# Two transformer blocks on one core: x's second half waited for later, pairs of weight units ended one after the other, pool mixing on four PSUM tiles

## The chip, the cores and the metric

The kernel runs on one NeuronCore of a Trainium2 chip. The metric is the device time of one execution in microseconds (us). Five engines work side by side: TensorE (PE, matrix products), VectorE (DVE), ScalarE (ACT), GpSimd (POOL) and SyncE (SP, which here only issues transfers). They meet through semaphores.

## The reference

The program computes two different blocks, each two layers deep, for 512 tokens of 1024 channels in float32. The first block also carries a context stream of 256 tokens, so that in its first layer each product runs over 768 tokens, and in its second layer over 512.

```python
for l in range(DEPTH):                       # first block
    ml = ada_mod(c, w_ada[l], b_ada[l], 6)   # modulation vectors
    hl = modulate(x, ml[..., 0, :], ml[..., 1, :])
    zl = hl @ w_in[l] + b_in[l]              # q, k, v, conv, pool input, gates
    ...
    outs.append(win_sum / cnt - uf[:, :, sl])                 # multiscale pool, 4 windows
    mixed = jnp.einsum('blgi,gio->blgo', pooled, pool_w)      # the mixing, 4 groups of 256 channels
    m = gates[..., 0, :] * attn_o + gates[..., 1, :] * conv_o + gates[..., 2, :] * pool_o
    x = layer_norm(ALPHA * x + ml[..., 2, :] * (m @ w_out + b_out))
    x = layer_norm(ALPHA * x + ml[..., 5, :] * ffn(modulate(x, ml[..., 3, :], ml[..., 4, :])))
for i in range(DEPTH):                       # second block
    u = rmsnorm(h, ln_mix[i]) @ w_in[i]
    h = h + jnp.concatenate([y_mla, y_gla], axis=-1) @ w_out[i]
    gate = jax.nn.sigmoid(rmsnorm(h, ple_norm[i]) @ w_ple_gate[i])
    h = h + gate * (p[i] @ w_ple_proj[i])
```

## The kernel before

**Products.** Activations stand with channels on the partitions, in 8 chunks of 128. Each float32 product is made of three passes: high half of the weights by high half of the activations (`WH`, `XH`), low by high (`WL`, `XH`), high by low (`WH`, `XL`). A weight *unit* holds 8 blocks of 128 x 128, so one unit gives one output chunk. Units go through a ring of 4 slots: SP loads them into one of two raw buffers, ACT writes the high half (`weight_hi`, L1176, semaphore `hi_done`), and POOL (L464) or, in two stages, DVE (`low_half`, L1856) writes the low half (`units_split`). PE counts `units_used`.

**PSUM.** There are four tiles of 1024 columns. `tile_free[t]` counts their releases by ACT or DVE. `STAGES` lists for each stage of the program how often it uses each tile, from which `taken` and `emptied` work out the counts to wait for. Most stages alternate between two tiles: unit n of a stage waits until unit n-2 has been read out.

**Pairs.** Where a stage begins before its activations are all there, the first two units are computed together, chunk by chunk: `first_pair` in the first block (L503; stages conv, pw, out, up0, down0, down1, down2, so 7 in each layer) and `paired` in the second block (L842; ina, w_out, pg). For each chunk k the order is pass 0 of both units, pass 1 of both, pass 2 of both. The third unit then needs the tile of the first (in ina it has another tile).

**Mixing (L798).** For each of the 4 pool groups PE makes two output chunks, on tiles 0 and 1; ACT (L1410) reads both out when both are done. The groups' inputs (`pooled`) come from DVE's `pool_windows`.

**Entry.** SP issues 16 pieces of the modulation weights (512 KB each), the small tables, two weight units and then x in two halves (L417). PE sums the modulation vectors (L674), ACT copies the sums (`ada_copy`, L1315), PE turns them (`ada_turned`, L684), DVE adds the bias (L1997), and then ACT and DVE make the high and low halves of the first stage's input (L1330, L2135, L2141), and the first pair runs (L503). PE's wait ahead of `ada_turned` is

```python
pe.wait_ge(loaded, 6 * 16)
```

and `loaded` counts the five small tables and x's second half. Behind the first pair PE makes two more modulation steps (`ada_ahead`, L674), whose last weights come into `tmp`, a buffer that is free once the low halves of all 8 chunks are written.

Of the kernel before, what the change touches and what calls it, by code (L numbers as in the profile page):

```python
# [24 lines left out]
P = 128  # L25
# [32 lines left out]
X_AT = ({j: (2 * j - 6, 2 * j - 5) for j in range(3, 7)}, {2: (0, 1), 3: (2, 3), 4: (4, 5), 5: (6, 7)})  # L58
UQ_ITEMS = (4, 5, 0, 1, 2, 3, "rope0", "rope1", "rope2", 6, 7, 8, 9, 10, 11, 12, 13)
# [22 lines left out]
for _l in range(LAYERS):  # L82
    if _l == 0:
        STAGES += [((_l, "ada"), 0, (0, 0, 0, 1))]
    STAGES += [((_l, "ada_rest"), 0, (0, 0, 1, 1)), ((_l, "conv"), 4, (8, 8, 0, 0)), ((_l, "gate0"), 2, (4, 4, 0, 0)),
               ((_l, "qkv"), 3, (6, 6, 3, 10)), ((_l, "attn"), 0, (16, 16, 32, 16))]
    if _l == 0:
        STAGES += [((_l, "attn_ctx"), 0, (8, 8, 16, 8))]
    STAGES += [((_l, "u"), 2, (4, 4, 0, 0)), ((_l, "mix"), 0, (4, 4, 0, 0)), ((_l, "gate2"), 2, (4, 4, 0, 0)), ((_l, "cln"), 0, (0, 0, 2, 2)),
               ((_l, "gate1"), 2, (4, 4, 0, 0)), ((_l, "pw"), 2, (0, 0, 4, 4)), ((_l, "out"), 2, (4, 4, 0, 0)),  # L90
               ((_l, "ln1"), 0, (1, 0, 2, 1))]
# [39 lines left out]
def two_blocks(nc, weights, ada_w, pool_w, vec1_d, vec2_d, gla_w_d, x_d, cond_d, ple_d, pos_d, consts_d, rope_d,  # L131
# [4 lines left out]
    with ctx:  # L136
# [132 lines left out]
        cond_loaded, loaded = sem("conditions_loaded"), sem("params_loaded")  # L269
# [116 lines left out]
        def _(sp):  # L386
# [71 lines left out]
        def _(pool):  # L458
# [7 lines left out]
            for r0, r1 in ((RING[0, "conv"], RING[0, "conv"] + 1), (RING[0, "qkv"] + 1, RING[1, "conv"] + 1), (RING[1, "qkv"] + 1, ROUNDS)):  # L466
                if r0:
                    pool.wait_ge(units_split, r0 * SLOTS)
# [6 lines left out]
        def _(pe):  # L475
            def linear(l, st, rounds, sp_, kt=CH, hi=XH, lo=XL, ready=None, ahead=None, behind=None, within=None, by_chunk=False, tb=0):
# [17 lines left out]
                def first_pair():  # L494
                    start(0, 0)
                    start(0, 1)
                    for k in range(kt):
                        for n, (w, act) in enumerate(((WH, hi), (WL, hi), (WH, lo))):
                            if n != 1:
                                pe.wait_ge(*at_least(l, ready[n // 2][0], ready[n // 2][1] + k + 1))  # L500
                            for s in range(2):
                                for a, b in sp_:
                                    last = nc.tensor.matmul(ps(tb + s, a, b), w[:, s * UNIT + k * P:s * UNIT + (k + 1) * P],  # L503
                                                            act[:, k * TOK + a:k * TOK + b],
                                                            start=(n == 0 and k == 0), stop=(n == 2 and k == kt - 1))
                                if n == 2 and k == kt - 1:
                                    last.then_inc(units_used, 1)
# [214 lines left out]
            def block1(l):  # L722
                sp_, W = spans(l), width(l)
                if l == 0:
# [6 lines left out]
                    pe.wait_ge(loaded, 6 * 16)  # L731
# [59 lines left out]
                for g in range(4):  # L791
                    pe.wait_ge(*at_least(l, "pooled", 2 * g + 2))
                    for o in range(2):
                        pe.wait_ge(tile_free[o], taken(l, "mix", o, g))
                        for k in range(2):
                            w0 = POOLW + ((2 * g + o) * 2 + k) * P
                            for a, b in sp_:
                                last = nc.tensor.matmul(ps(o, a, b), AR[:, w0:w0 + P],  # L798
# [38 lines left out]
            def block2(l):  # L837
# [6 lines left out]
                def paired(st, hi, lo, n, ks, ready, before=None):  # L844
# [4 lines left out]
                    for at_, k in enumerate(ks):  # L849
                        if before:  # L850
                            before(k)
                        for i, (w, act) in enumerate(((WH, hi), (WL, hi), (WH, lo))):
                            if i == 0:
                                pe.wait_ge(*at_least(l, ready[0], ready[2](k)))
                            if i == 2:
                                pe.wait_ge(*at_least(l, ready[1], ready[2](k)))
                            for s in range(2):
                                last = products(ps(s, 0, SEQ), w, act, slot_of(l, st, s) * UNIT + k * P, n, k, i == 0 and at_ == 0, i == 2 and at_ == CH - 1)
                                if i == 2 and at_ == CH - 1:
                                    last.then_inc(units_used, 1)  # L860
# [303 lines left out]
        def _(act):  # L1164
# [642 lines left out]
            for s in range(2):  # L1807
# [11 lines left out]
        def _(dve):  # L1819
# [294 lines left out]
            def block1(l):  # L2114
                W = width(l)
                if l == 0:
                    dve.wait_ge(on(0, "ada_image"), 1)
# [8 lines left out]
                if l == 0:  # L2126

                    dve.wait_ge(x_half, 16)
                    for i in range(CH // 2):
                        if i == CH // 4:  # L2130
                            dve.wait_ge(loaded, 6 * 16)
# [661 lines left out]
```

## Time and profile before

| | |
|---|---|
| median of 3 runs | 3341.41 us (3340.28 to 3343.42) |
| profiled execution | 3340.82 us |
| its span, first to last instruction | 3339.0 us |
| mean granted clock of TensorE | 0.981 of 2.4 GHz |
| busy: PE / DVE / ACT / POOL | 96% / 59% / 34% / 25% |

The profiled execution's time is its span and 1.8 us around it. Busy time is an average over stages. Idle time of PE is listed in the trace with the operation whose end released it; an operation behind which a chain hangs moves with everything ahead of it.

### The profile page before, as it was taken

How to read it: one execution, taken by the hardware profiler on the slowest of the kernel's cores; microseconds unless marked ns; L12 is line 12 of the kernel's file. 1: busy time of each engine (PE TensorE's matmuls, PEld its weight loads, DVE VectorE, ACT ScalarE, POOL GpSimd, SP SyncE). 2: the span in 40 equal slices, each digit the busy share in tenths (PEclk: the TensorE clock that was granted, in tenths of full speed). 3: DMA queues.
4: the chain of work that ended last, by engine and by line, in shares of the span. 5: the costliest groups of instructions: out<-in, count | busy, mean ns of one | idle time of the engine just before them, and what ended most of it. 6: DMA issues, size and time to landing. Idle time of an engine off the chain costs nothing.

```text
span 3339.0 us, 43512 instructions
## 1 busy us (share of the span) xinstructions
PE 3207.3 (96%) x16010; PEld 2520.0 (75%) x16010; DVE 1953.8 (59%) x2687; ACT 1138.2 (34%) x1615; POOL 848.3 (25%) x336
## 2 busy tenths in 40 slices
PE   6999999999989999998999999999999999999998
PEld 4778777788878888886777767688886776777765
DVE  4887886654566253457888885583466525344333
ACT  2122254233233121223234435442225334442433
POOL 1001201233323232230020134354443231332312
PEclk8999999999999999999999999999999899999999
DMA  7442101112111111124520023232322210221211
GB/s 269 161 168 76 51 1 32 44 57 101 57 46 61 64 63 63 63 69 167 209 78 26 32 75 114 73 99 91 96 92 85 70 63 21 93 82 51 70 38 63
DMA packets 75307, 270.50 MB, mean 81 GB/s; under 512 B 8592, under 2 KB 9616, under 8 KB 74512
## 3 DMA queue, kind: packets, MB, share of 16 engines
q1 hardware_dynamic: 71376, 256.04, 23.0%
q10 hardware_dynamic: 3776, 12.32, 1.0%
q8 instruction: 107, 1.75, 0.2%
q14 instruction: 48, 0.39, 0.0%
HBM read 263.87 MB, written 4.46 MB: 80 GB/s over the span
## 4 chain that ended last, share of the span: by engine, by line
PE 85%; DVE 8%; DVEq 2%; ACT 2%; issue 1%; DMA 1%; SPq 0%; ACTq 0%
PE ps L537 48%; PE ps L842 12%; PE ps L503 4%; PE ps L653 2%; PE ps L776 2%; PE ps L983 1%; DVE arena L2061 1%; PE ps L953 1%; PE ps L674 1%; PE ps L641 1%; PE ps L798 1%; DVE x L2069 1%; PE ps L1062 1%; PE ps L756 1%; PE ps L1082 1%
## 5 line engine op out<-in xcount | busy, mean ns | idle before, releaser
L464 POOL TENSOR_TENSOR w_lo<-w_raw,w_hi 128x1024 fp32r<-128x1024 f32 x332 | 848.1, 2558 | 2455.2 <-ACT w_hi L1176 2455.1
L1176 ACT ACTIVATE w_hi<-w_raw 128x1024 fp32r<-128x1024 f32 x380 | 399.1, 1054 | 556.0 <-PE ps L537 297.2
L537 PE MATMUL ps<-act_hi,w_hi 128*128 128x512 f32 (+1 forms) x2608 | 552.3, 361 | 7.6 <-ACT arena L1410 1.8
L537 PE MATMUL ps<-act_lo,w_hi 128*128 128x512 f32 (+1 forms) x2608 | 536.2, 355 | 0.0
L537 PE MATMUL ps<-act_hi,w_lo 128*128 128x512 f32 (+1 forms) x2608 | 535.3, 354 | 0.0
L537 PEld LDWEIGHTS ps<-act_hi,w_hi 128*128 128x128 f32 x2608 | 427.7, 188 | 126.8 <-issue 50.9
L537 PEld LDWEIGHTS ps<-act_hi,w_lo 128*128 128x128 f32 x2608 | 428.3, 188 | 72.5
L537 PEld LDWEIGHTS ps<-act_lo,w_hi 128*128 128x128 f32 x2608 | 428.3, 188 | 72.4 <-issue 0.5
L1909 DVE SCALAR_TENSOR_TENSOR x<-ps,mod,x 128x512 f32<-128x512 f32 x96 | 60.2, 659 | 295.5 <-PE ps L537 238.2
L2069 DVE SCALAR_TENSOR_TENSOR x<-arena,vec,x 128x512 f32<-128x512 f32 x336 | 230.5, 714 | 0.0
L2061 DVE SCALAR_TENSOR_TENSOR arena<-arena,vec 128x783 f32<-128x783 f32 (+1 forms) x240 | 228.0, 950 | 0.2 <-issue 0.2
L2292 DVE SCALAR_TENSOR_TENSOR arena<-arena,vec 128x769 f32<-128x769 f32 (+1 forms) x88 | 160.4, 1823 | 16.0 <-issue 16.0
L1242 ACT ACTIVATE arena<-ps,vec 128x768 f32<-128x768 f32 (+3 forms) x64 | 50.8, 794 | 281.5 <-PE ps L537 195.1
L842 PE MATMUL ps<-act_hi,w_hi 128*128 128x512 f32 x432 | 127.5, 432 | 9.2 <-ACT act_hi L1522 6.2
L1830 DVE TENSOR_TENSOR ffn_lo<-arena,ffn_hi 128x768 f32 (+1 forms) x44 | 119.0, 2704 | 6.5
L842 PEld LDWEIGHTS ps<-act_hi,w_hi 128*128 128x128 f32 x432 | 86.3, 206 | 38.6 <-issue 19.8
L842 PE MATMUL ps<-act_hi,w_lo 128*128 128x512 f32 x432 | 112.8, 395 | 0.0
L842 PE MATMUL ps<-act_lo,w_hi 128*128 128x512 f32 x432 | 111.6, 392 | 0.0
L776 PE MATMUL ps<-arena 128*128 128x256 f32 (+1 forms) x288 | 102.4, 475 | 5.9 <-ACT tmp L1281 5.9
L2289 DVE TENSOR_SCALAR arena<-arena,vec 128x769 f32<-128x769 f32 (+1 forms) x44 | 29.1, 661 | 132.4 <-ACT arena L1494 132.4
L1494 ACT ACTIVATE arena<-ps 128x512 f32<-128x512 f32 x66 | 32.4, 526 | 213.8 <-PE ps L537 211.1
L653 PE MATMUL ps<-arena 128*128 128x256 f32 x416 | 103.1, 381 | 1.6 <-ACT arena L1398 1.5
(336 smaller groups left out, 4494.5 us busy)
## 6 DMA issues: line engine op xcount, KB each, us to landing
w_raw<-in_weights SPq DMA_DIRECT2D x380, 512.0 KB, 3.5
arena<-in_ada_w SPq DMA_DIRECT2D x75, 512.0 KB, 4.6
tmp<-in_ada_w SPq DMA_DIRECT2D x21, 512.0 KB, 4.4
x<-in_x SPq DMA_DIRECT2D x2, 1536.0 KB, 19.9
x<-in_x ACTq DMA_DIRECT2D x1, 3072.0 KB, 10.8
arena<-in_pool_w ACTq DMA_DIRECT2D x2, 1024.0 KB, 4.9
x_mid<-x ACTq DMA_DIRECT2D x1, 2048.0 KB, 7.4
x<-x_mid ACTq DMA_DIRECT2D x1, 2048.0 KB, 8.5
```

The costliest lines, as they stand in the source:

```text
L464: nc.gpsimd.tensor_tensor(WL[:, w], raw, WH[:, w].bitcast(f32), ALU.subtract).then_inc(units_split, 1)
L503: last = nc.tensor.matmul(ps(tb + s, a, b), w[:, s * UNIT + k * P:s * UNIT + (k + 1) * P], act[:, k * TOK + a:k * TOK + b], start=(n == 0 ...
L537: last = nc.tensor.matmul(ps(t, a, b), w[:, s * UNIT + k * P:s * UNIT + (k + 1) * P], act[:, k * TOK + a:k * TOK + b], start=(n == 0 and k ...
L653: last = nc.tensor.matmul(ps(3, (m % 2) * 512, (m % 2) * 512 + 2 * P), values(m, k), AR[:, a:a + 2 * P], start=(k == 0), stop=(k == nk - 1))
L776: last = nc.tensor.matmul(ps(it % 2, a, b), AR[:, q:q + P], AR[:, k + a:k + b], start=True, stop=True)
L842: return nc.tensor.matmul(out, w0[:, k0:k0 + P], act[:, k * n:k * n + SEQ], start=start, stop=stop)
L1176: nc.scalar.activation(WH[:, s * UNIT:(s + 1) * UNIT], RAW[:, (s % 2) * UNIT:(s % 2 + 1) * UNIT], ACT.Copy).then_inc(hi_done, 1)
L1830: return V.tensor_tensor(lo, src, hi.bitcast(f32), ALU.subtract)
L1909: last = V.scalar_tensor_tensor(x, ps(t, a, b), at(MOD, mod(l, gate, j, m), 1), x, ALU.mult, ALU.add)
L2061: t = V.scalar_tensor_tensor(acc, src, w, acc, ALU.mult, ALU.add)
L2069: t = V.scalar_tensor_tensor(acc, src, w, acc, ALU.mult, ALU.add)
L2292: t = V.scalar_tensor_tensor(cv, src, w, cv, ALU.mult, ALU.add)
```

## The change

It has four parts.

1. x's second half is counted on the semaphore of the conditions (`cond_loaded`) and no longer on `loaded`. PE waits for the five tables alone ahead of `ada_turned`; ACT and DVE wait for the second half at chunk 4. SP waits for the conditions' activation before it issues x.
2. The low halves of the first four units go from POOL to DVE: two ahead of the modulation vectors, two behind the last low half of x. ACT makes the high half of unit 1 behind `ada_copy`.
3. In the last chunk of each pair the three passes of unit 0 come first, then the three of unit 1.
4. The mixing takes tiles 0 and 1 for even groups, 2 and 3 for odd ones.

```diff
+ORDER_OF_PAIR = (((0, 0), (0, 1), (1, 0), (1, 1), (2, 0), (2, 1)), ((0, 0), (1, 0), (2, 0), (0, 1), (1, 1), (2, 1)))
...
-    STAGES += [((_l, "u"), 2, (4, 4, 0, 0)), ((_l, "mix"), 0, (4, 4, 0, 0)), ...
+    STAGES += [((_l, "u"), 2, (4, 4, 0, 0)), ((_l, "mix"), 0, (2, 2, 2, 2)), ...
...
-            for k, landed in enumerate((x_half, loaded)):
+            sp.wait_ge(on(0, "cond"), 1)
+            for k, landed in enumerate((x_half, cond_loaded)):
...
-            for r0, r1 in ((RING[0, "conv"], RING[0, "conv"] + 1), (RING[0, "qkv"] + 1, RING[1, "conv"] + 1), (RING[1, "qkv"] + 1, ROUNDS)):
+            for r0, r1 in ((RING[0, "qkv"] + 1, RING[1, "conv"] + 1), (RING[1, "qkv"] + 1, ROUNDS)):
...
-                        for n, (w, act) in enumerate(((WH, hi), (WL, hi), (WH, lo))):
-                            if n != 1:
+                        for n, s in ORDER_OF_PAIR[k == kt - 1]:
+                            w, act = ((WH, hi), (WL, hi), (WH, lo))[n]
+                            if n != 1 and s == 0:
                                 pe.wait_ge(*at_least(l, ready[n // 2][0], ready[n // 2][1] + k + 1))
...
-                    pe.wait_ge(loaded, 6 * 16)
+                    pe.wait_ge(loaded, 5 * 16)
...
-                        pe.wait_ge(tile_free[o], taken(l, "mix", o, g))
+                        t = 2 * (g % 2) + o
+                        pe.wait_ge(tile_free[t], taken(l, "mix", t, g // 2))
...
-                        for i, (w, act) in enumerate(((WH, hi), (WL, hi), (WH, lo))):
+                        for i, s in ORDER_OF_PAIR[at_ == CH - 1]:
...
-                            act.wait_ge(loaded, 6 * 16)
+                            act.wait_ge(cond_loaded, 2 * 16)
...
-                    nc.scalar.activation(AR[:, B0 + c * TOK:B0 + c * TOK + W], ps(c % 2, 0, W), ACT.Copy,
-                                         scale=v1(l, "pool_scale", c)).then_inc(tile_free[c % 2], 1)
+                    nc.scalar.activation(AR[:, B0 + c * TOK:B0 + c * TOK + W], ps(c % 4, 0, W), ACT.Copy,
+                                         scale=v1(l, "pool_scale", c)).then_inc(tile_free[c % 4], 1)
...
-            for s in range(2):
-                weight_hi(0, s)
+            weight_hi(0, 0)
             ada_copy(0, False)
+            weight_hi(0, 1)
...
                 if l == 0:
+                    low_half(0)
+                    low_half(1)
                     dve.wait_ge(on(0, "ada_image"), 1)
...
+                    low_half(2)
+                    low_half(3)
```

The order on the engines, at three places. On DVE, at the start of the program, this stood ahead of the modulation vectors (`mod`):

```order
L2652 MEMSET ones_in_first_column 128x1
L1997 TENSOR_TENSOR mod<-ps,vec 128x32
L2003 TENSOR_SCALAR mod<-mod 128x16
L2121 TENSOR_SCALAR qk_bias<-vec 128x8
L2122 TENSOR_SCALAR qk_bias<-vec 128x2
```

and this stands there now:

```order
L2656 MEMSET ones_in_first_column 128x1
L1856 TENSOR_TENSOR w_lo<-w_raw,w_hi 128x1024 x2
L1997 TENSOR_TENSOR mod<-ps,vec 128x32
L2003 TENSOR_SCALAR mod<-mod 128x16
L2123 TENSOR_SCALAR qk_bias<-vec 128x8
L2124 TENSOR_SCALAR qk_bias<-vec 128x2
```

The low halves of units 0 and 1 have come in ahead of the vectors; those of units 2 and 3 stand in the same way between the last `act_lo` and the memset of the convolution's buffer.

On PE, the last chunk of the first pair of stage conv (two column spans, 512 and 256, for each unit and pass) was

```order
L503 MATMUL ps<-act_hi,w_hi 128x512
L503 MATMUL ps<-act_hi,w_hi 128x256
L503 MATMUL ps<-act_hi,w_hi 128x512
L503 MATMUL ps<-act_hi,w_hi 128x256
L503 MATMUL ps<-act_hi,w_lo 128x512
L503 MATMUL ps<-act_hi,w_lo 128x256
L503 MATMUL ps<-act_hi,w_lo 128x512
L503 MATMUL ps<-act_hi,w_lo 128x256
L503 MATMUL ps<-act_lo,w_hi 128x512
L503 MATMUL ps<-act_lo,w_hi 128x256
L503 MATMUL ps<-act_lo,w_hi 128x512
L503 MATMUL ps<-act_lo,w_hi 128x256
```

and is now

```order
L504 MATMUL ps<-act_hi,w_hi 128x512
L504 MATMUL ps<-act_hi,w_hi 128x256
L504 MATMUL ps<-act_hi,w_lo 128x512
L504 MATMUL ps<-act_hi,w_lo 128x256
L504 MATMUL ps<-act_lo,w_hi 128x512
L504 MATMUL ps<-act_lo,w_hi 128x256
L504 MATMUL ps<-act_hi,w_hi 128x512
L504 MATMUL ps<-act_hi,w_hi 128x256
L504 MATMUL ps<-act_hi,w_lo 128x512
L504 MATMUL ps<-act_hi,w_lo 128x256
L504 MATMUL ps<-act_lo,w_hi 128x512
L504 MATMUL ps<-act_lo,w_hi 128x256
```

The same twelve products; unit 0 ends behind the sixth of them and no longer behind the tenth.

On PE, the second and third group of the mixing in layer 0, with the semaphores that they wait for, began

```order
L798 MATMUL ps<-arena 128x512 [waits tile_free0,block0_pooled]
L798 MATMUL ps<-arena 128x256
L798 MATMUL ps<-arena 128x512
L798 MATMUL ps<-arena 128x256
L798 MATMUL ps<-arena 128x512 [waits tile_free1]
```

in both, and the second begins now

```order
L800 MATMUL ps<-arena 128x512 [waits tile_free2,block0_pooled]
L800 MATMUL ps<-arena 128x256
L800 MATMUL ps<-arena 128x512
L800 MATMUL ps<-arena 128x256
L800 MATMUL ps<-arena 128x512 [waits tile_free3]
```

while the third goes back to tiles 0 and 1. Only the tiles waited for have moved.

## Rows read from the trace of the kernel before

**Rows 1.** The page's chain that ended last, by engine

```profile
PE 85%; DVE 8%; DVEq 2%; ACT 2%; issue 1%; DMA 1%; SPq 0%; ACTq 0%
```

**Rows 2.** Waits of PE, whole span: total us, times, longest

```profile
PE ps L720 <- DVE arena L2177: 7.1, 4, 3.9
PE ps L537 <- DVE x L1909: 7.0, 8, 1.1
...
PE ps L798 <- ACT arena L1410: 5.9, 6, 1.1
...
PE ps L842 <- DVE arena L2630: 2.4, 3, 1.0
...
PE ps L537 <- ACT arena L1410: 1.8, 2, 1.0
PE ps L537 <- DVE arena L2230: 1.7, 2, 0.9
...
PE ps L842 <- DVE x L2613: 1.3, 2, 0.6
PE ps L537 <- ACT arena L1494: 1.3, 2, 0.7
...
PE ps L537 <- ACT arena L1345: 0.6, 1, 0.6
```

**Rows 3.** Timeline, 28 to 42 us: start, length, engine; idle before and releaser

```profile
28.90 1.06 ACT L1176 ACTIVATE w_hi<-w_raw 128x1024 fp32r<-128x1024 f32 x1 [0.21 <-DMA w_raw<-in_weights]
...
29.99 0.60 ACT L1315 ACTIVATE arena<-ps 128x512 f32<-128x512 f32 x1
...
37.02 1.88 PE L684 MATMUL ps<-ident,arena 128*128 128x8 f32 x8 [7.11 <-DMA x<-in_x]
...
41.08 1.62 PE L503 MATMUL ps<-act_hi,w_hi 128*128 128x512 f32 x4 [2.18 <-ACT act_hi L1330]
```

**Rows 4.** SP's two transfers of x: starts, and issue to landing

```profile
L417 SPq DMA_DIRECT2D x<-in_x x2: 433/1458/2483, 14.6 to 15.1; - x2
...
DMA to landing us min/median/max: 17.9/19.9/21.9
```

**Rows 5.** Timeline, 44 to 66 us, the first pair and what follows

```profile
44.09 1.65 DVE L2135 TENSOR_SCALAR tmp<-x,mod 128x512 f32<-128x512 f32 x4
...
50.45 5.65 POOL L464 TENSOR_TENSOR w_lo<-w_raw,w_hi 128x1024 fp32r<-128x1024 f32 x2 [16.86 <-ACT w_hi L1176]
...
51.39 5.64 DVE L2135 TENSOR_SCALAR tmp<-x,mod 128x512 f32<-128x512 f32 x4
...
58.12 0.96 PE L503 MATMUL ps<-act_lo,w_hi 128*128 128x512 f32 x4 [0.82 <-DVE act_lo L2141]
...
61.13 1.06 PE L674 MATMUL ps<-arena,gla_w 128*32 128x512 f32 x8
63.01 0.62 PE L674 MATMUL ps<-arena,gla_w 128*32 128x512 f32 x2 [0.81 <-DMA tmp<-in_ada_w]
...
64.01 3.09 PE L537 MATMUL ps<-act_hi,w_hi 128*128 128x512 f32 x16
...
65.97 1.22 DVE L1856 TENSOR_TENSOR w_lo<-w_raw,w_hi 128x1024 fp32r<-128x1024 f32 x1
```

**Rows 6.** The page's DMA issues: count, KB each, us to landing

```profile
tmp<-in_ada_w SPq DMA_DIRECT2D x21, 512.0 KB, 4.4
```

**Rows 7.** Timeline, last chunk of up0's pair in layer 0

```profile
959.23 0.87 PE L503 MATMUL ps<-act_hi,w_lo 128*128 128x512 f32 x4
...
959.94 0.86 PE L503 MATMUL ps<-act_lo,w_hi 128*128 128x512 f32 x4
```

**Rows 8.** Timeline, the mixing: layer 0, then layer 1

```profile
620.19 5.40 PE L798 MATMUL ps<-arena 128*128 128x512 f32 x16 [1.08 <-ACT arena L1410]
...
1949.64 0.24 DVE L2110 TENSOR_TENSOR arena<-arena 128x8 f32<-128x8 f32 x2
...
1952.15 3.67 PE L798 MATMUL ps<-arena 128*128 128x512 f32 x8 [0.87 <-ACT arena L1410]
```

More of the change, by code:

```diff
@@ L88 @@
         STAGES += [((_l, "attn_ctx"), 0, (8, 8, 16, 8))]
-    STAGES += [((_l, "u"), 2, (4, 4, 0, 0)), ((_l, "mix"), 0, (4, 4, 0, 0)), ((_l, "gate2"), 2, (4, 4, 0, 0)), ((_l, "cln"), 0, (0, 0, 2, 2)),
+    STAGES += [((_l, "u"), 2, (4, 4, 0, 0)), ((_l, "mix"), 0, (2, 2, 2, 2)), ((_l, "gate2"), 2, (4, 4, 0, 0)), ((_l, "cln"), 0, (0, 0, 2, 2)),
                ((_l, "gate1"), 2, (4, 4, 0, 0)), ((_l, "pw"), 2, (0, 0, 4, 4)), ((_l, "out"), 2, (4, 4, 0, 0)),
@@ L266, in in2 @@
             return "inb", m, m % 2, m // 2 + (m > 6)
[L269 removed]
+        cond_loaded, loaded = sem("conditions_and_then_rest_of_x_loaded"), sem("params_loaded")
         x_half = sem("first_half_of_x_loaded")
@@ L464, in low_half @@
                 nc.gpsimd.tensor_tensor(WL[:, w], raw, WH[:, w].bitcast(f32), ALU.subtract).then_inc(units_split, 1)
-            for r0, r1 in ((RING[0, "conv"], RING[0, "conv"] + 1), (RING[0, "qkv"] + 1, RING[1, "conv"] + 1), (RING[1, "qkv"] + 1, ROUNDS)):
-                if r0:
-                    pool.wait_ge(units_split, r0 * SLOTS)
+            for r0, r1 in ((RING[0, "qkv"] + 1, RING[1, "conv"] + 1), (RING[1, "qkv"] + 1, ROUNDS)):
+                pool.wait_ge(units_split, r0 * SLOTS)
                 with loop(pool, r1 - r0) as r:
@@ L497, in first_pair @@
                     for k in range(kt):
-                        for n, (w, act) in enumerate(((WH, hi), (WL, hi), (WH, lo))):
-                            if n != 1:
+                        for n, s in ORDER_OF_PAIR[k == kt - 1]:
+                            w, act = ((WH, hi), (WL, hi), (WH, lo))[n]
+                            if n != 1 and s == 0:
                                 pe.wait_ge(*at_least(l, ready[n // 2][0], ready[n // 2][1] + k + 1))
-                            for s in range(2):
[L502 to L507, printed above, removed]
+                            for a, b in sp_:
+                                last = nc.tensor.matmul(ps(tb + s, a, b), w[:, s * UNIT + k * P:s * UNIT + (k + 1) * P],
+                                                        act[:, k * TOK + a:k * TOK + b],
+                                                        start=(n == 0 and k == 0), stop=(n == 2 and k == kt - 1))
+                            if n == 2 and k == kt - 1:
+                                last.then_inc(units_used, 1)
                 if ready:
@@ L797, in block1 @@
                             for a, b in sp_:
-                                last = nc.tensor.matmul(ps(o, a, b), AR[:, w0:w0 + P],
+                                last = nc.tensor.matmul(ps(t, a, b), AR[:, w0:w0 + P],
                                                         AR[:, B0 + (2 * g + k) * TOK + a:B0 + (2 * g + k) * TOK + b],
@@ L851, in paired @@
                             before(k)
-                        for i, (w, act) in enumerate(((WH, hi), (WL, hi), (WH, lo))):
[L853 to L860, printed above, removed]
+                        for i, s in ORDER_OF_PAIR[at_ == CH - 1]:
+                            w, act = ((WH, hi), (WL, hi), (WH, lo))[i]
+                            if i != 1 and s == 0:
+                                pe.wait_ge(*at_least(l, ready[i // 2], ready[2](k)))
+                            last = products(ps(s, 0, SEQ), w, act, slot_of(l, st, s) * UNIT + k * P, n, k, i == 0 and at_ == 0, i == 2 and at_ == CH - 1)
+                            if i == 2 and at_ == CH - 1:
+                                last.then_inc(units_used, 1)
                 def single(st, i, t, k_use, hi=XH, lo=XL, n=TOK, within=None):
@@ L1806, in _ @@
                                  ACT.Silu).then_inc(on(0, "cond"), 1)
-            for s in range(2):
-                weight_hi(0, s)
+            weight_hi(0, 0)
             ada_copy(0, False)
+            weight_hi(0, 1)
             act.dma_start(AR[:, COS:COS + 2 * SEQ], rope_d).then_inc(on(0, "rope_table"), 16)
@@ L2130, in block1 @@
                         if i == CH // 4:
-                            dve.wait_ge(loaded, 6 * 16)
+                            dve.wait_ge(cond_loaded, 2 * 16)
                         dve.drain()
```

## Prediction

> **What bounds the kernel now.** I read the chain that ended last first: 85% of the span hangs on PE, 8% on DVE [rows 1]. So an edit is worth what it takes out of PE's idle time, provided that nothing behind PE is late by itself. The second view is the list of PE's waits [rows 2]. Three groups in it belong to this change. Behind the pairs PE waits for the tile of unit 0: 7.0 us in 8 places for the residual, 1.7 in 2 for the merge, 1.3 in 2 for up0's copy, 0.6 in 1 for conv in layer 1, and in the second block 1.3 in 2 and two of the three waits on L2630. In the mixing it waits 5.9 us in 6 places for ACT's read-out, and 1.8 in 2 more at the first unit of gate2 behind it, which uses tile 0 too. The third view is the timeline of the entry: PE stands 7.11 us ahead of `ada_turned`, released by a transfer of x, though ACT's copy of the sums was over at 29.99 + 0.60 = 30.59 [rows 3].
>
> Not all waits are open to the change. L720's 7.1 us [rows 2] is time in which PE waits for DVE's norms; they begin only when PE hands them work, so I take that stretch to move as a whole.
>
> **Entry, up to the first pair.** What holds `ada_turned` falls away: of x's two halves, issued at 14.6 and 15.1, one landed 17.9 us and the other 21.9 us after its issue [rows 4]. In order that is 32.5 and 37.0, and 37.02 is when PE went on. The turning can start at 30.6 and ends 1.88 later, at 32.5. DVE now stands with two low halves ahead of the modulation vectors. The second needs ACT's high half of unit 1, now behind the copy: 30.59 + 1.06 = 31.65, and DVE's 1.22 [rows 3, 5] make 32.87, some 0.3 us later than PE's 32.5 and the hand-over. Queued behind it on DVE are the vectors, and on these wait ACT and PE. The gap from the end of the turning to the first pair was 41.08 - 38.90 = 2.18; so the pair starts at about 32.6 + 2.2 = 34.8 to 34.9, against 41.08: **6.2 us**. x's first half (32.5) is there before ACT asks for it; the second (37.0) is for chunk 4, which PE, at 2.1 us a chunk or more (three times the 0.71 of [rows 7]), does not reach before 43. SP's new wait on the conditions costs nothing: PE's sums, which ACT copies at 29.99, need the same activation, and the transfers issued ahead of x kept the queue busy until x landed.
>
> **Entry, the pair itself.** One chunk's low half held PE until 58.12, and the fourth part of the input on DVE had taken 5.64 where the part before took 1.65, beside two POOL operations of 5.65 together [rows 5]. POOL has nothing to do there now, so DVE gets 4.0 back. Chunk 6's low half would be ready at 58.12 - 4.0 - 6.2 = 47.9 and the last at about 48.9, well ahead of PE, which comes to the last chunk 2.1 us ahead of the pair's end, near 52. That gives the 0.82 us and the idle crumbs around it, about 1.0. The page SBUF — State Buffer of the Trainium skill (section Who interferes with whom) says that a DVE operation with two-port access and a GpSimd operation exclude each other for a whole instruction; the 5.64 agrees. The pair ends at 61.13 - 6.2 - 1.0 = 53.9.
>
> Behind the lows DVE makes the low halves of units 2 and 3, 1.22 each: 50.1 and 51.4. PE's third unit starts later than that, so cover is 3.8 us. But SP's next weight load waits for the first of them, and behind it in SP's queue stand the two modulation pieces that PE needs right behind the pair. The last went into `tmp` and held PE 0.81 us already [rows 5]. It would now be issued at about 50.2 + 0.6 + 0.6 = 51.5 and take 4.4 (the median of its kind [rows 6]): 55.9. PE gets there at 53.9 + 1.1 = 55.0, so a wait of 0.9 stays. PE's third unit then starts at about 56.9 in place of 64.01: **the entry gives 7.1 us**. If the piece lands at once, 7.9; if three transfers in a row take a microsecond longer, 6.1.
>
> **Pairs.** In layer 0, four products of the last chunk take 959.94 - 959.23 = 0.71 us [rows 7], so unit 0's last two and the same of unit 1 take 0.355 each. Before, unit 0 ended one such step ahead of the pair's end, now three: its tile comes free 0.71 earlier. The waits there are 0.65 to 1.1 [rows 2], so nearly all of it counts: 0.7 in pw, out, up0 and the three downs, 6 x 0.7 = 4.2. Conv in layer 0 has the modulation steps behind its pair and gives nothing. With 512 columns it is two thirds, 0.47: 7 pairs in layer 1, 4 of the second block's 6 (ina has another tile), 11 x 0.47 = 5.1, below each wait there. Sum **9.3**, of the 13 or so us waited. The low half of the last chunk is wanted one step and a half earlier, but where PE runs closest behind DVE, in up0, it went straight through [rows 7]. If the chunk's low half were late, that pair would give back up to 0.7.
>
> **Mixing.** The wait for tiles 0 and 1 goes where the group before used the other two: 3 x 1.08 + 1.0 = 4.2 us in layer 0, since a group's 5.40 us covers ACT's read-out of the group before [rows 2, 8]. In layer 1 it is 5.9 - 3.2 = 2.7 and 0.8. What is late next there is `pooled`: DVE ends the last chunk at 1949.88 [rows 8]; the fourth group began at 1952.15 and would like to begin 3 x 0.87 = 2.6 earlier, at 1949.5. So 0.4 comes back as a wait on DVE: 3.1. Sum **7.3**; DVE's taps behind gate2 begin with gate2's first read-out and move along.
>
> **Sum.** 7.1 + 9.3 + 7.3 = 23.7. The profiled execution (3340.82) goes to 3317.1; it stood 0.6 below the median, so I say **3317.7**. Its own range is 3314 to 3321: entry 6.1 to 7.9, pairs 8 to 9.3, mixing 6.5 to 7.7, and 1.5 us of spread between runs.
>
> **Rivals.**
> - *x's first half lands no earlier than the second* (10%). The four microseconds between the landings are read off two transfers [rows 4]. The page DMA: Bandwidth & Descriptors of the Trainium skill (section Queues, rings and completion order) says that completion is not in order of issue. As a mechanism here: the halves share the queue with the last weights, both are complete at 37.0, and ACT starts then. The pair starts at 37.0 + 2.2 = 39.2, the entry gives 1.9 + 1.0 = 2.9, and the time is 3321.9. For it: only the sum of the waits speaks, no engine waited for the first half. Against it: the two latencies, 17.9 and 21.9.
> - *The pairs and the mixing give half* (10%). Where DVE or ACT has a chain of its own behind the pair, an earlier tile only makes PE wait elsewhere. For it: L720's 7.1 us and the mixing's `pooled`. Against it: PE's waits end with the tile's read-out, and the read-outs start when PE's unit ends. Half of 16.6 is 8.3: 3326.0.
> - *Slower* (3%). In the stages where PE waits for DVE, each meeting of DVE with a POOL operation stretches a DVE operation by some 2 us (5.64 against 1.65 for two meetings [rows 5]). Moved phases could make more of them. It takes 12 new ones on the path to cancel 23.7, and 15 to be slower by over 0.2%, to 3348. POOL's work is released by ACT and this by PE, so they move together; that is why I give it little.
> - *The rest of the forecast* (77%) is the sum above.
>
> **Range and chances.** 0.2% is 6.7 us, about what a measurement of this kernel tells from none. 3313 to 3326 takes in the first two rivals' centres and all bounds. Faster 0.94, within 0.2% 0.03, slower 0.03.
>
> **What would show it.** `ada_turned` at 30.6 to 31 with no wait on x; the first pair at 34.8, DVE's four input parts all at 1.65 and no wait on `act_lo`; PE's third unit near 57. Waits behind the pairs of 0.2 to 0.4 in place of 0.7 to 1.1, in 17 places. No wait on L1410 in the mixing, one of 0.4 on DVE ahead of the last group in layer 1. The forecast is wrong if the act_hi of chunk 0 waits for x beyond 33, if PE waits for `units_split` at its third unit, or if the waits of rows 2 on L2177, L2021 or L1203 grow by what the others lose.

## The result and the profile after

| | before | after |
|---|---|---|
| median | 3342.41 us (3340.28 to 3344.83, 4 runs) | 3318.60 us (3317.08 to 3319.36, 4 runs) |
| profiled execution | 3340.82 us | 3319.36 us |
| its span | 3339.0 us | 3317.6 us |

The ratio is 0.993, 95% interval 0.9919 to 0.9942: faster by 0.7%. The medians lie 23.8 us apart (forecast 23.7; forecast time 3317.7, measured 3318.60), the two profiled executions 21.5 and their spans 21.4.

First the waits of PE in the changed kernel (total us, times, longest; L numbers are lines of the changed kernel, a few higher than in [rows 2]), against [rows 2].

```profile
PE ps L721 <- DVE arena L2181: 7.3, 4, 4.1
...
PE ps L675 <- DMA tmp<-in_ada_w: 3.9, 2, 2.2
...
PE ps L538 <- DVE x L1909: 2.3, 8, 0.4
...
PE ps L844 <- DVE arena L2634: 1.5, 3, 1.0
...
PE ps L800 <- DVE arena L2110: 0.7, 1, 0.7
...
PE ps L538 <- DVE arena L2234: 0.6, 2, 0.3
...
PE ps L844 <- DVE act_lo L2363: 0.4, 1, 0.4
...
PE ps L538 <- ACT arena L1345: 0.4, 1, 0.4
...
PE ps L844 <- DVE x L2617: 0.4, 2, 0.2
```

The eight waits for the residual fell from 7.0 to 2.3, the merge's two from 1.7 to 0.6, up0's copy (1.3) is gone, and so are both waits for the mixing's read-out (5.9 and 1.8). The norms' wait stayed, as said: 7.3 against 7.1. New are 0.7 in the mixing for the pool inputs and 0.4 in the first pair of the second block for a low half.

The timeline of the entry, 26 to 44 us (start, length, engine; idle before and releaser), against [rows 3]:

```profile
28.62 0.58 ACT L1315 ACTIVATE arena<-ps 128x512 f32<-128x512 f32 x1
...
29.34 1.03 PE L685 MATMUL ps<-ident,arena 128*128 128x8 f32 x8 [1.10 <-ACT arena L1315]
...
32.60 9.82 ACT L1330 ACTIVATE act_hi<-x,mod 128x512 fp32r<-128x512 f32 x16 [2.46 <-DMA x<-in_x]
...
34.05 1.62 PE L504 MATMUL ps<-act_hi,w_hi 128*128 128x512 f32 x4 [3.68 <-ACT act_hi L1330]
```

PE turns the vectors at 29.34 and waits for ACT's copy alone; before it went on at 37.02. ACT now has to wait for x's first half, which lands at 32.5 as in the kernel before. By the transfers' own group the two halves took as long as in [rows 4], within 0.4 us:

```profile
L419 SPq DMA_DIRECT2D x<-in_x x2: 432/1464/2495, 14.7 to 15.1; - x2
...
DMA to landing us min/median/max: 17.8/20.1/22.3
```

The timeline of the first pair's second half and what follows, 44 to 60 us, against [rows 5]:

```profile
43.68 1.65 DVE L2137 TENSOR_SCALAR tmp<-x,mod 128x512 f32<-128x512 f32 x4
...
47.16 2.35 DVE L1856 TENSOR_TENSOR w_lo<-w_raw,w_hi 128x1024 fp32r<-128x1024 f32 x2
...
49.73 0.33 SPq L391 DMA_DIRECT2D tmp<-in_ada_w  x1
...
52.67 1.06 PE L675 MATMUL ps<-arena,gla_w 128*32 128x512 f32 x8
...
55.94 0.62 PE L675 MATMUL ps<-arena,gla_w 128*32 128x512 f32 x2 [2.20 <-DMA tmp<-in_ada_w]
...
56.93 3.08 PE L538 MATMUL ps<-act_hi,w_hi 128*128 128x512 f32 x16
```

DVE's last part takes 1.65 and no longer 5.64, the low halves of units 2 and 3 follow at 47.16, and PE's third unit starts at 56.93 against 64.01.

The mixing, layer 0 and layer 1, in PE's timeline, against [rows 8]:

```profile
610.52 14.78 PE L800 MATMUL ps<-arena 128*128 128x512 f32 x45
...
1924.47 10.46 PE L800 MATMUL ps<-arena 128*128 128x512 f32 x24
1935.58 3.70 PE L800 MATMUL ps<-arena 128*128 128x512 f32 x8 [0.66 <-DVE arena L2110]
```

No gap is left in layer 0, and in layer 1 one, ahead of the last group, for DVE. Layer 0's first mixing product and the first product of gate2 behind it, in the kernel before:

```profile
613.78 5.33 PE L798 MATMUL ps<-arena 128*128 128x512 f32 x16
...
639.54 3.08 PE L537 MATMUL ps<-act_hi,w_hi 128*128 128x512 f32 x16 [0.99 <-ACT arena L1410]
```

The changed one starts gate2 here:

```profile
630.97 3.13 PE L538 MATMUL ps<-act_hi,w_hi 128*128 128x512 f32 x16
```

From start to start that is 25.76 us before and 20.45 (630.97 - 610.52) now, 5.31 less, though the waits taken out are 3 x 1.08 + 0.99 = 4.23.

Last, the span cut at the same two points of the program (PE's third unit of layer 1's first stage, and the first product of the second block). Behind the bounds stand the length, the busy time of PE, of its weight loads, DVE, ACT and POOL, and then the granted clock. The kernel before,

```profile
0.00:1534.06 1534.06, 1464.16 (x8165) 1202.82 (x8165) 919.43 (x1234) 448.11 (x600) 327.31 (x128) 0.99 0.24 81
1534.06:2538.88 1004.82, 969.90 (x4368) 750.60 (x4369) 694.70 (x877) 368.97 (x499) 309.00 (x120) 0.99 0.29 97
```

and the changed one:

```profile
0.00:1519.78 1519.78, 1463.92 (x8165) 1204.66 (x8165) 919.81 (x1238) 448.57 (x600) 324.65 (x124) 0.99 0.24 82
1519.78:2518.86 999.08, 969.32 (x4368) 751.14 (x4369) 692.01 (x877) 369.02 (x499) 309.39 (x120) 0.99 0.29 98
```

PE (the number behind the length) was busy for the same time in both, to 0.6 us. The first part is 14.28 us shorter and PE's idle time in it 14.0, the second part 5.74 and 5.2. What is left of the 21.4 lies behind, 1.4: the second block's products take 2.4 less, and the exit 1.0 more, because its last two products took 2.08 in place of 1.12. So in sum the two executions differ by idle time; the granted clock moved a few microseconds between stretches, in both directions, as is shown below.

### The profile page after: what moved, and what is told of

Its sections match the earlier page's. It is cut to its first block, busy times and chain, and to the rows that moved or that the text cites. A ratio compares the mean times of both kernels' runs of the same rounds, so it can differ in the third digit from the quotient of the medians.

```text
span 3317.6 us, 43566 instructions
## 1 busy us (share of the span) xinstructions
PE 3206.8 (97%) x16010; PEld 2521.2 (76%) x16010; DVE 1949.2 (59%) x2691; ACT 1138.4 (34%) x1615; POOL 846.1 (26%) x332
## 4 chain that ended last, share of the span: by engine, by line
PE 85%; DVE 9%; DVEq 2%; ACT 2%; issue 1%; DMA 1%; SPq 0%; ACTq 0%
PE ps L538 48%; PE ps L844 12%; PE ps L504 4%; PE ps L654 2%; PE ps L777 2%; PE ps L983 1%; DVE arena L2061 1%; PE ps L675 1%; PE ps L642 1%; PE ps L953 1%; DVE x L2069 1%; PE ps L1062 1%; PE ps L757 1%; PE ps L1082 1%; PE ps L587 1%
## 5 line engine op out<-in xcount | busy, mean ns | idle before, releaser
L1909 DVE SCALAR_TENSOR_TENSOR x<-ps,mod,x 128x512 f32<-128x512 f32 x96 | 60.3, 659 | 291.3 <-PE ps L538 238.2
```

Source lines behind the costliest of these rows:

```text
L1909: last = V.scalar_tensor_tensor(x, ps(t, a, b), at(MOD, mod(l, gate, j, m), 1), x, ALU.mult, ALU.add)
```

## The experiments

Medians are compared with the kernel before, timed beside each group of versions: 3341.86 us (28 runs) for the first four, 3340.48 (9 runs) for the next four, 3341.33 (9) for the three after them, 3340.89 (7) for the last.

**The entry alone.** The order of the pairs and the mixing stay as before.

```diff
-ORDER_OF_PAIR = (((0, 0), (0, 1), (1, 0), (1, 1), (2, 0), (2, 1)), ((0, 0), (1, 0), (2, 0), (0, 1), (1, 1), (2, 1)))
+ORDER_OF_PAIR = (((0, 0), (0, 1), (1, 0), (1, 1), (2, 0), (2, 1)), ((0, 0), (0, 1), (1, 0), (1, 1), (2, 0), (2, 1)))
```

> The entry alone (semaphores of x, low halves of the first four units on DVE, the high half of unit 1 behind the copy of the sums); pairs and mixing as before. Theory (the three parts add up, each worth the idle time it takes from PE): 7.1 us less than the kernel before, PE's third unit of stage conv starting at 56.9 us. Rival (the entry's gain is eaten in the attention of layer 0, where the changed kernel was seen to lose 2.5 us of its lead): 4.6 us less, with the lead shrinking between 380 and 415 us. A second rival, that the parts interact: less than 4 us or more than 10.

3336.77 us (11 runs), ratio 0.9981, interval 0.9972 to 0.9991: 5.1 us between medians, 6.3 by the ratio. The interval, 3.0 to 9.4 us, holds both the theory's 7.1 and the rival's 4.6; what decides between them is under "The sum by parts" below. Its timeline around the pair:

```profile
30.68 1.03 PE L685 MATMUL ps<-ident,arena 128*128 128x8 f32 x8 [0.82 <-ACT arena L1314]
...
34.72 1.62 PE L504 MATMUL ps<-act_hi,w_hi 128*128 128x512 f32 x4 [3.00 <-ACT act_hi L1329]
...
51.08 0.33 SPq L391 DMA_DIRECT2D tmp<-in_ada_w  x1
...
54.03 1.06 PE L675 MATMUL ps<-arena,gla_w 128*32 128x512 f32 x8
...
57.29 0.62 PE L675 MATMUL ps<-arena,gla_w 128*32 128x512 f32 x2 [2.19 <-DMA tmp<-in_ada_w]
```

Turning, pair and pair's end stand where the prediction put them (30.6, 34.8, 53.9). The piece in `tmp` doesn't: issued at 51.08 (forecast 51.5), PE could use it 6.2 us later, not 4.4. The third unit starts at 58.28.

**The order of the pairs alone.**

```diff
+ORDER_OF_PAIR = (((0, 0), (0, 1), (1, 0), (1, 1), (2, 0), (2, 1)), ((0, 0), (1, 0), (2, 0), (0, 1), (1, 1), (2, 1)))
...
-                        for n, (w, act) in enumerate(((WH, hi), (WL, hi), (WH, lo))):
-                            if n != 1:
+                        for n, s in ORDER_OF_PAIR[k == kt - 1]:
+                            w, act = ((WH, hi), (WL, hi), (WH, lo))[n]
+                            if n != 1 and s == 0:
```

> The order inside the last chunk of each pair alone; entry and mixing as before. Theory: 9.3 us less than the kernel before, PE's waits on L1909 down from 7.0 to about 2.3 us and those behind the other pairs to 0.2 to 0.4 each. Rival (DVE or ACT has a chain of its own behind the pairs): half or less, about 4.6 us, with other waits of PE longer.

3335.30 us (11 runs), ratio 0.9978 (0.9969 to 0.9987): 7.4 us by the ratio, with 4.3 to 10.4 in the interval, so the forecast 9.3 and the rival's 4.6 both fit the time, and the waits have to decide. PE's waits behind the pairs are those of the full change (the eight on x fell to 2.3 here too):

```profile
PE ps L843 <- DVE arena L2629: 1.5, 3, 1.0
...
PE ps L538 <- DVE arena L2229: 0.6, 2, 0.3
...
PE ps L538 <- ACT arena L1344: 0.5, 1, 0.5
...
PE ps L843 <- DVE x L2612: 0.4, 2, 0.2
```

**The mixing alone.**

```diff
-    STAGES += [((_l, "u"), 2, (4, 4, 0, 0)), ((_l, "mix"), 0, (4, 4, 0, 0)), ...
+    STAGES += [((_l, "u"), 2, (4, 4, 0, 0)), ((_l, "mix"), 0, (2, 2, 2, 2)), ...
...
-                        pe.wait_ge(tile_free[o], taken(l, "mix", o, g))
+                        t = 2 * (g % 2) + o
+                        pe.wait_ge(tile_free[t], taken(l, "mix", t, g // 2))
```

> The four tiles in the mixing alone. Theory: 7.3 us less than the kernel before (4.2 in layer 0, 3.1 in layer 1), no wait of PE on ACT's read-out in the mixing, and one of 0.4 to 0.7 us on DVE's pooled input ahead of the last group of layer 1. Rival (what is won comes back at the next wait on DVE, the sums of the convolution in layer 1, where PE waits 1.0 us): 4.2 us less and that wait at about 4 us.

3331.63 us (6 runs), ratio 0.9969 (0.9956 to 0.9981): 10.4 us by the ratio, the forecast 7.3 inside its interval (6.3 to 14.7 us). The rival's wait for the convolution's sums stayed at 1.0. The mixing of layer 1:

```profile
1934.67 10.46 PE L799 MATMUL ps<-arena 128*128 128x512 f32 x24
1946.01 3.70 PE L799 MATMUL ps<-arena 128*128 128x512 f32 x8 [0.88 <-DVE arena L2111]
```

The three ratios add up to 24.1 us, the full change gives 23.4 by its own: no sign that the parts lean on one another, within what three intervals of 3 to 4 us each way can tell.

**The entry's semaphores alone.** x's second half is waited for later, but the low halves of the first four units stay on POOL and ACT's order stays.

```diff
-            for k, landed in enumerate((x_half, loaded)):
+            sp.wait_ge(on(0, "cond"), 1)
+            for k, landed in enumerate((x_half, cond_loaded)):
...
-                    pe.wait_ge(loaded, 6 * 16)
+                    pe.wait_ge(loaded, 5 * 16)
```

> The entry's semaphores alone: x's second half no longer holds the turning of the sums; the low halves of the first four units stay on POOL and ACT's order stays. Theory (the 5.6 us operation on DVE beside POOL costs, apart from the wait on x): 6.3 us less than the kernel before, with PE waiting about 0.8 us for act_lo and DVE's fourth part of the input again at 5.6. Rival (the low halves on POOL cost nothing, the wait on x is all): the same as the whole entry, 7.1 us less, third unit at 56.9.

3335.54 us (11 runs), ratio 0.9981 (0.9972 to 0.999), the same as the whole entry; an interval of 3.3 to 9.4 us can't part the theory's 6.3 from the rival's 7.1. Its timeline:

```profile
29.15 4.65 POOL L466 TENSOR_TENSOR w_lo<-w_raw,w_hi 128x1024 fp32r<-128x1024 f32 x2 [28.70 <-ACT w_hi L1176]
...
32.36 1.47 DVE L2003 TENSOR_SCALAR mod<-mod 128x16 f32<-128x16 f32 x1
...
35.44 1.62 PE L505 MATMUL ps<-act_hi,w_hi 128*128 128x512 f32 x4 [3.47 <-ACT act_hi L1330]
...
45.75 5.62 DVE L2135 TENSOR_SCALAR tmp<-x,mod 128x512 f32<-128x512 f32 x4
...
53.49 0.33 SPq L391 DMA_DIRECT2D tmp<-in_ada_w  x1
...
57.02 0.62 PE L676 MATMUL ps<-arena,gla_w 128*32 128x512 f32 x2 [0.49 <-DMA tmp<-in_ada_w]
...
58.02 2.26 PE L539 MATMUL ps<-act_hi,w_hi 128*128 128x512 f32 x11
```

With POOL at work the pair starts 0.7 later and DVE's fourth part takes 5.62 again, so the piece for `tmp` is issued 2.4 later than with the low halves on DVE. But it lands after 3.4 us in place of 6.1, and PE waits 0.49 for it in place of 2.19. The third unit starts at 58.02, 0.3 ahead of the kernel with the whole entry. So neither the theory nor the rival had it: the 5.6 us operation costs in the pair, and taking it away gained nothing, because the transfer behind gave all of it back.

**The changed kernel with units 2 and 3 back on POOL.**

```diff
+            pool.wait_ge(units_split, 2)
+            for s in (2, 3):
+                low_half(0, s)
...
-                    low_half(2)
-                    low_half(3)
```

> The changed kernel with the low halves of units 2 and 3 on POOL again (units 0 and 1 stay on DVE). Theory, from the runs of the entry (the third unit began at 58.3 us with all four on DVE and at 58.0 with all four on POOL): what DVE wins in the pair comes back as a longer wait for the modulation piece in tmp, so the third unit starts within 0.6 us of the changed kernel's 56.9, DVE's fourth part of the input again taking 5.6 and the wait for tmp about 1 us shorter. Rival (the forecast's): DVE's 4 us count, PE waits 0.8 us for act_lo and the third unit comes 1 us or more later, near 58.

3317.42 us (5 runs), ratio 0.993 (0.9917 to 0.9944), that of the change itself. Its third unit starts at 57.70, between the theory's bound (57.5) and the rival's 58; DVE's fourth part takes 5.66, PE waits 0.52 for `act_lo` and 0.55 for the piece. But in this profile the pair began only at 35.07, against 34.05, because PE's last modulation sums ran at the lower clock (2.77 us for ten products against 1.48). From the pair's start to the third unit it is 22.6 us here, 22.9 in the changed kernel: the same trade once more.

**The changed kernel with the two modulation pieces ahead of the weight load** in SP's queue, at the one step where both stand.

```diff
-                        unit_load(r + (RING[l, st] + (s + 3) // SLOTS), (s + 3) % SLOTS)
+                        ada_first = l == 0 and st == "conv" and s == 1
+                        if not ada_first:
+                            unit_load(r + (RING[l, st] + (s + 3) // SLOTS), (s + 3) % SLOTS)
...
+                        if ada_first:
+                            unit_load(r + (RING[l, st] + (s + 3) // SLOTS), (s + 3) % SLOTS)
```

> The changed kernel with two transfers exchanged in SP's queue: the two modulation pieces that PE needs behind the first pair go ahead of the weight unit that waits for the low half of unit 2. Theory (the 2.2 us wait for tmp is the queue behind that unit's wait and transfer): the piece is issued at about 47.3 us and lands near 51.3, the wait is gone, the third unit starts at 54.8, and the whole is 2.1 us less than the changed kernel. Rival (the unit loaded later is missed instead): no gain, with PE waiting for a unit of stage conv or ACT's high halves late by more than 3 us.

3315.80 us (5 runs), ratio 0.9922 (0.9908 to 0.9935). The piece is issued at 47.56, lands 3.5 us later and nobody waits for it:

```profile
47.56 0.33 SPq L391 DMA_DIRECT2D tmp<-in_ada_w  x1
...
52.59 1.48 PE L679 MATMUL ps<-arena,gla_w 128*32 128x512 f32 x10
...
54.44 3.10 PE L542 MATMUL ps<-act_hi,w_hi 128*128 128x512 f32 x16
```

The third unit starts 2.5 us earlier than in the changed kernel (56.93), with the pair at the same place. So it was the transfer that held it. This profile does not carry the lead to the end: in the norms of layer 1 PE waited 2.7 us that most profiles don't have (10.0 in 5 places on the norms, where the changed kernel has 7.3 in 4), and it came to the second block at 2519.1, as the changed kernel did; a second profile of the same version, below, came there at 2513.3.

**The changed kernel with the last two chunks by unit** in the pairs where a wait was left (pw, out, the downs, w_out, pg).

```diff
-                    for k in range(kt):
-                        for n, s in ORDER_OF_PAIR[k == kt - 1]:
+                    by_unit = 2 if tb == 2 or st == "out" else 1
+                    steps = [(k, n, s) for k in range(kt - by_unit) for n, s in ORDER_OF_PAIR[0]]
+                    steps += [(k, n, s) for s in range(2) for k in range(kt - by_unit, kt) for n in range(3)]
+                    for k, n, s in steps:
...
+                    by_unit = 1 if st == "ina" else 2
```

> The changed kernel with the last two chunks of the pair by unit instead of the last one, in stages pw, out, the downs, w_out and pg. Theory (each remaining wait behind a pair is the rest of the read-out that three more products of 128 x 512 hide): PE's waits on L1909, on the merge, on w_out's and on pg's residual go from 3.8 us together to under 0.5, and the time is 3.5 us less than the changed kernel. Rival (the chunks' low halves come too late for unit 0 where DVE is close): new waits for act_lo or ffn_lo of as much.

3316.75 us (5 runs), ratio 0.9925 (0.9911 to 0.9938): the waits on L1909 and L2234 are gone, with them 2.9 us, those on the second block's residuals too (two of three on L2634, both on L2617), as the theory has it, 0.4 more came at `act_lo`, and the median moved by less than the runs' spread and not by 3.5. The second block's products (first and last start behind the colon), in the changed kernel and in this one:

```profile
L844 PE MATMUL ps<-act_hi,w_hi x432: 387/393/796, 2518.9 to 3233.1; 128*128 128x512 f32 x144
```

```profile
L846 PE MATMUL ps<-act_hi,w_hi x432: 387/389/796, 2511.1 to 3234.6; 128*128 128x512 f32 x144
```

It enters the second block 7.8 us ahead, more than the 2.9 of the waits and so partly for other reasons (two profiles of the version before it were 5.8 apart here), and leaves it 1.5 behind. The granted clock (the third number from the right) tells where most of it went, in the same two kernels:

```profile
3000.00:3100.00 100.00, 99.62 (x507) 79.19 (x508) 30.05 (x58) 26.05 (x39) 20.61 (x10) 0.86 0.15 48
```

```profile
3000.00:3100.00 100.00, 99.62 (x481) 79.07 (x480) 26.35 (x53) 25.62 (x39) 18.80 (x8) 0.80 0.12 43
```

PE is busy throughout in both, but ran longer at the lower of its two levels, and got through fewer instructions. Such windows of fixed time hold somewhat different work in each kernel. Cut by work, the products that the kernel before makes from 3000 to 3100 us took 106.0 us in this kernel at a clock of 0.84, and 100.1 in the changed one at 0.90, as in the kernel before (100.0 at 0.90).

**Both additions together.**

> Both: the two transfers exchanged and the last two chunks by unit. Theory: the gains add, 5.6 us less than the changed kernel, about 3313. Rival: less than 3 us, with the difference in a stage where PE's clock was granted low or in a new wait.

3315.05 us (5 runs), ratio 0.992 (0.9906 to 0.9933): not the 3313 of gains that add. The stretch just named took 106.0 us here too, at 0.84.

**Three kernels side by side**, since the versions above were not timed beside the change: the changed kernel, the one with both additions, and the one with the earlier pieces alone.

> The changed kernel once more, in one call with the version that has all four parts and two additions. Expected 3318 to 3319 us, some 23 us below the kernel before, with its third unit at 56.9 again.

> The changed kernel with the two modulation pieces ahead of the weight load in SP's queue and two chunks by unit where the pair's waits were left. If the piece in the temporary buffer was what held the third unit (2.2 us of waiting) and the tiles' read-outs the rest (2.3 + 0.6 + some 1 us), it is 5 to 6 us below the changed kernel of this call; the first reading gave 3.5 us between medians of two calls. If the third unit only moves a wait to a later place, as the rival has it, the difference is under 2 us. The kernel that has the first addition alone should stand 2.5 us below the changed kernel by its third unit, 54.44 against 56.93.

> The changed kernel with the two modulation pieces ahead of the weight load in SP's queue alone: 2.5 us below the changed kernel of this call if the 2.5 us at the third unit last to the end, 0 if the norms of DVE or the exit take them back.

The changed kernel took 3317.03 us (3316.09 to 3318.47), with both additions 3314.45 (3313.63 to 3316.93), with the earlier pieces alone 3314.02 (3312.58 to 3318.14); 5 runs each. The earlier pieces give 3.0 us between medians against the 2.5 expected, though the ranges overlap, and in these two profiles the third unit stood 1.3 apart (56.75 and 55.42), not 2.5. With both additions it is 2.6, neither the 5 to 6 of the theory nor the rival's under 2: the two chunks give nothing on top.

**Two chunks by unit in the first block alone**, with the earlier pieces.

```diff
-                    by_unit = 1 if st == "ina" else 2
+                    by_unit = 1
```

> The version with both additions, but with two chunks by unit in the first block's pairs alone; the second block's pairs keep the change's order. In the kernel with both, PE came to the second block 2.1 us ahead of the one without the two chunks (2511.2 against 2513.3) and left its last products 1.4 us behind it (3228.7 against 3227.3), while the granted clock from 3000 to 3100 us was 0.83 against 0.87. If the order inside the second block's pairs lowers that clock, it goes back to 0.86 or 0.87 here and the time falls to about 3312. If it is only where the phases of the second block come to stand, which the earlier arrival alone decides, the clock stays at 0.83 there and the time at 3314 to 3315.

3311.88 us (3309.39 to 3314.20, 4 runs), ratio 0.991 (0.9894 to 0.9927): the lowest median of all versions, 29.0 us below the kernel before timed beside it. The interval overlaps that of the earlier pieces alone (0.991 to 0.9937), so it isn't shown to be faster than they are. From 3000 to 3100 us the kernel with both additions (first fence) had 0.83, this one (second) 0.86:

```profile
3000.00:3100.00 100.00, 99.62 (x474) 78.38 (x473) 25.64 (x51) 25.69 (x38) 19.00 (x9) 0.83 0.13 47
```

```profile
3000.00:3100.00 100.00, 99.62 (x498) 78.81 (x499) 26.78 (x54) 27.69 (x41) 21.57 (x10) 0.86 0.14 48
```

This is what the theory of the order inside the second block's pairs expected, in clock and in the median. The profiled execution itself was the slowest of the four (3314.20, against 3314.45 for the profile with both additions), so clock and gain were not seen in one execution. By work the evidence is stronger: the products of that stretch took 104.5 to 106.0 us in the three profiles with two chunks in the second block, at 0.84 to 0.85, and 99.9 to 100.1 in all eleven others, this version's among them, at 0.90. The rival is not out. The three came to the second block at 2511.0 to 2511.2 us, the eleven between 2513.3 and 2538.9, this version at 2513.3; no kernel with the change's order arrived as early as the three.

## Why the prediction held, and where a size was off

**Turning and pair.** Right. x's first half was there at 32.5 and the second did not matter: the rival of halves that land together is out (the two halves landed apart in all 14 profiles, after 17.8 to 17.9 and 21.7 to 22.3 us). The full change turned 1.3 us earlier than said (29.34), with PE's last modulation sums run at the full clock in that execution (ten products in 1.48 us, in the kernel before 2.77); ACT then stood against x's first half, so only 0.75 of it reached the pair (34.05). In the entry alone the turning came at 30.68 and the pair at 34.72, as forecast.

**The pair itself.** I put its gain at 1.0. The pair, from its start up to the modulation step at 52.67, took 18.6 us against 20.05: 1.4. In the entry alone it took 19.3: 0.7. DVE's four parts are all 1.65 in both and neither waits for `act_lo`; the changed kernel's clock rose 0.4 us sooner in the second chunk, and its products then followed each other 2% faster.

**Behind the pair: the term that was mis-sized.** "Take 4.4 (the median of its kind)", and from it "a wait of 0.9 stays". The piece for `tmp` was issued at 49.73, 1.8 ahead of my 51.5, since DVE was done earlier. It took 6.2, not 4.4, and landed at 55.9, to the tenth what I had. PE came 1.3 earlier than I had it, and so it waited 2.2. Two errors of 1.8 cancelled in the landing, and with it in the third unit: 56.93 against 56.9. The entry alone shows the size without the luck: PE at the place forecast, 6.2 from the issue to PE's start, a wait of 2.19 and the third unit at 58.28, 1.4 late. 4.4 is the median of 21 transfers of its kind in one profile, and not even this piece's own time there, 3.7. By the landing itself the same piece took 5.6 to 6.2 in the four profiles where it is issued 0.6 us behind another piece and 1.2 behind a weight load, all of 512 KB, and 3.4 to 3.7 in the ten where everything ahead of it was issued 4.8 us or more before. A duration taken from a median has to be one of transfers with the same neighbours.

**Pairs.** Right in place, and in size by the waits: these are 0.2 to 0.4 in 15 places and gone in two (up0's copy). The one of conv in layer 1 fell from 0.64 to 0.44 alone, where I took off 0.47: unit 0 was done at 1518.65, but ACT was issuing a transfer (L1514) until 1518.90 and read out from 1518.95. New is that ina's pair waits 0.44 for a low half, at 2526.53 in its fourth chunk, which the new order doesn't touch: that product starts 7.67 us behind the pair's start in both kernels, and in the changed one PE's clock rose some 1 us earlier in the pair, so it stood waiting. By time the pairs alone gave 7.4 us, known to 3 us each way, so the 9.3 is not confirmed to better than that.

**Mixing: right in the waits, and worth more than I said.** Layer 0 runs without a gap and gains 5.31 us where I had 4.2. I counted PE's idle time alone. Without the wait the groups also follow each other more closely: 20.45 us for four is 5.11 each, where the profile has 5.33 to 5.40 busy for one that ends at a wait. In layer 1 the same: three groups take 10.46 in place of 3 x 3.67. From the first mixing product to gate2 it is 14.25 in the changed kernel and 14.48 with the mixing alone, 17.99 before: 3.7 and 3.5 for my 3.1. So the mixing gives 8.8 to 9.1 us by its starts where I forecast 7.3, and 10.4 by its time. For the same reason PE is at `pooled` earlier than I had it, and waits 0.66 (0.88 with the mixing alone) instead of 0.4.

**The sum by parts.** Up to layer 1's third unit I had 7.1 + 4.2 + 4.2 + 0.47 = 16.0, the two profiles differ by 14.28; from there to the second block 3.1 + 6 x 0.47 = 5.9 against 5.74; behind it 1.9 against 1.4. Three things make the first part. The mixing gave 1.1 more than forecast. PE's lead of 7.05 us at the first norms (383.58 against 390.63) shrank to 4.53 at 541.74, and to 3.26 at the mixing (610.52 against 613.78), in stretches that the change does not touch. And from gate2 to the end of the part it gained 5.7, with 4.67 forecast for the pairs there; but the three versions with the old order of the pairs gained 1.9 to 3.5 on the kernel before over the same products, so that profile was slow there, and the 5.7 doesn't measure the pairs. From 370 to 430 us the kernel before had, and the changed one has:

```profile
370.00:430.00 60.00, 51.82 (x312) 42.35 (x312) 47.30 (x74) 21.47 (x31) 10.04 (x4) 0.97 0.12 36
```

```profile
370.00:430.00 60.00, 51.74 (x295) 41.91 (x294) 44.15 (x74) 20.98 (x33) 7.80 (x3) 0.91 0.10 34
```

The entry alone, the pairs alone and the mixing alone had 0.91 there too, the entry's semaphores alone 0.94, and so had the four versions of the changed kernel that were timed next. The pairs alone and the mixing alone have the old entry, and they too lost 2.3 us on the kernel before between those two points, so the loss is not the entry's doing: that answers the rival of the entry alone. 0.97 was seen once in these profiles, in the kernel before. The medians don't hang on one execution; they say 23.8.

**How good the sum is.** Its closeness, 23.7 to 23.8, is in part luck. By their times the three parts are 6.3, 7.4 and 10.4 us where I had 7.1, 9.3 and 7.3. The mixing was worth more and the entry's third unit came later than the terms say; whether the pairs gave less, an interval of 4.3 to 10.4 doesn't tell.

**The rivals.** Halves that land together: refuted by ACT's start at 32.60. Half of pairs and mixing: refuted for the mixing, 10.4 us where half would be 3.7; for the pairs, 7.4 where half would be 4.6, the lower bound is 4.3, so this rests on the waits. Slower by more meetings of DVE and POOL: POOL's busy time is 846 us against 848 and DVE's 1949 against 1954. It did not happen. The waits named as signs of being wrong stayed or fell: 7.3 against 7.1 on the norms, 13.2 and 13.2 on L2021, 22.4 against 23.6 on L1203. The page SBUF — State Buffer of the Trainium skill (section Who interferes with whom) says that DVE in two-port access and GpSimd exclude each other for a whole instruction; five kernels here agree with it, 5.62 to 5.66 us for DVE's fourth part with POOL at work and 1.65 without.

## What to carry to other kernels

Passes reordered in the last chunk of a pair, or a second pair of tiles, add no work and take out the wait in front of the read-out; the waits are a first measure of their worth, not an exact one (in the mixing of layer 0 waits of 4.23 us went and 5.31 were gained). Where an engine is cleared, look in the queue behind it for the transfer that now decides: here low halves moved off POOL gave nothing while the pieces stood behind the weight load, and with these exchanged the third unit came 1.3 to 2.5 us earlier. (The exchange with the low halves left on POOL was not run.) And where PE is busy throughout, a version with fewer waits can be granted a lower clock, so such an edit is judged by time and clock together, not by waits.

## What the runs showed that was not expected

- The same stretch, with the same work, was granted 0.91, 0.94 or 0.97 of full clock in different executions (370 to 430 us). With 0.91 in place of 0.97 the lead shrank by 2.5 us.
- A DVE operation of 16 columns took 1.47 us beside a POOL operation and 0.17 without.
- The transfer of 512 KB into `tmp` took 5.6 to 6.2 us close behind two others of its size and 3.4 to 3.7 us where what went ahead was issued 4.8 us before or more.
- A wait taken out of the mixing was worth more than its idle time, because the products behind it also start closer together: 5.31 us for 4.23.
- Two chunks by unit in the second block's pairs went with 104.5 to 106.0 us for work that took 100 in every other version, at 0.84 to 0.85 of full clock instead of 0.90. Whether the order or the earlier arrival does it is open.
